# A second triangular inverse kept beside the first in an RWKV-7 chunk kernel: products on TensorE in place of transposes on VectorE

## The reference

```python
def rwkv7_scan(r, w, k, v, kk, a):
    def step(state, inp):
        r_t, w_t, k_t, v_t, kk_t, a_t = inp
        sa = jnp.einsum('bhvk,bhk->bhv', state, -kk_t)
        state = (state * w_t[:, :, None, :] + sa[..., None] * (kk_t * a_t)[:, :, None, :]
                 + v_t[..., None] * k_t[:, :, None, :])
        return state, jnp.einsum('bhvk,bhk->bhv', state, r_t)
    ...
# for each direction d (d = 1 on flipped sequences):
        o = rwkv7_scan(*ins)
        bonus = jnp.sum(rh * kd * r_k.astype(F32), axis=-1, keepdims=True) * vh
        dir_out.append((group_norm(o, gn_w, gn_b) + bonus.reshape(nB, S, D)) * g.astype(F32))
```

## Time and profile before

| | |
|---|---|
| median of three runs | 2423.7 us (2422.42 to 2425.13) |
| the profiled execution, its span | 2422.42 us, 2420.5 us |
| busy: TensorE, its weight loads | 2271.3 us (94%), 1695.2 us (70%) |
| busy: VectorE, ScalarE, GpSimd | 1254.5 (52%), 948.3 (39%), 829.2 (34%) us |
| the eight passes of `pair` | 906.7 to about 1392 us of the span, 485 us |

### The profile page before, as it was taken

One profiled execution on the slowest core, in us unless ns is written; L12 is line 12 of the kernel. 1 busy time (PEld: TensorE's weight loads), 2 busy tenths in 40 slices (PEclk: granted clock), 3 DMA queues, 4 the chain that ended last, 5 costly groups with the idle time before them and its releaser, 6 DMA issues.

```text
span 2420.5 us, 45998 instructions
## 1 busy us (share of the span) xinstructions
PE 2271.3 (94%) x19396; PEld 1695.2 (70%) x19396; DVE 1254.5 (52%) x2027; ACT 948.3 (39%) x1665; POOL 829.2 (34%) x456
## 2 busy tenths in 40 slices
PE   8999999999978998888888898999998999999998
PEld 6886778888866647777777747877887766763476
DVE  5128254022164476777777515595313899736123
ACT  4238434233244434454445434465322222344133
POOL 2310334344413124444444203344441433330246
PEclk9999999999979998999999999999997999999999
DMA  4312222232312210000000112244221333222222
GB/s 143 118 51 77 70 70 87 104 96 82 101 36 67 96 41 10 7 8 10 8 9 10 38 61 71 94 182 139 96 87 61 131 113 113 87 87 79 70 89 85
DMA packets 49883, 180.69 MB, mean 75 GB/s; under 512 B 5601, under 2 KB 5857, under 8 KB 49441
## 3 DMA queue, kind: packets, MB, share of 16 engines
q1 hardware_dynamic: 46064, 166.89, 21.0%
q10 hardware_dynamic: 3632, 11.08, 1.1%
HBM read 167.39 MB, written 10.55 MB: 74 GB/s over the span
## 4 chain that ended last, share of the span: by engine, by line
PE 72%; issue 12%; DVE 6%; ACT 6%; POOL 3%; DMA 1%; POOLq 0%; ACTq 0%; SPq 0%; DVEq 0%
PE ps L596 15%; PE ps L597 15%; PE ps L598 14%; PE ps L599 6%; POOL ring_lo L2202 3%; PE ps L895 3%; PE ps L858 2%; PE ps L644 2%; PE ps L886 1%; PE ps L806 1%; PE ps L1072 1%; PE ps L715 1%; ACT arena L1453 1%; PE ps L1008 1%; PE ps L730 1%
## 5 line engine op out<-in xcount | busy, mean ns | idle before, releaser
L2202 POOL TENSOR_TENSOR ring_lo<-ring,ring_hi 128x1024 fp32r<-128x1024 f32 x232 | 565.2, 2444 | 1017.7 <-ACT ring_hi L1129 1017.6
L598 PE MATMUL ps<-u_lo,ring_hi 128*128 128x512 f32 x968 | 384.8, 398 | 0.0
L1129 ACT ACTIVATE ring_hi<-ring 128x1024 fp32r<-128x1024 f32 x232 | 243.1, 1053 | 108.4 <-DMA ring<-in_wall 105.0
L599 PE MATMUL ps<-arena,ring 128*128 128x512 f32 x608 | 266.1, 594 | 6.3 <-ACT arena L1573 3.3
L599 PEld LDWEIGHTS ps<-arena,ring 128*128 128x128 f32 x608 | 114.4, 190 | 154.2 <-issue 138.5
L596 PE MATMUL ps<-mlp_u_hi,ring_hi 128*128 128x512 f32 x512 | 204.9, 400 | 13.0 <-DVE u_lo L1690 8.5
L598 PEld LDWEIGHTS ps<-u_lo,ring_hi 128*128 128x128 f32 x968 | 183.8, 190 | 43.4
L596 PE MATMUL ps<-mid_hi,ring_hi 128*128 128x512 f32 x512 | 203.4, 397 | 2.6 <-POOL ring_lo L2202 2.6
L597 PE MATMUL ps<-mlp_u_hi,ring_lo 128*128 128x512 f32 x512 | 203.7, 398 | 0.0
L598 PE MATMUL ps<-mid_lo,ring_hi 128*128 128x512 f32 x512 | 202.6, 396 | 0.0
L597 PE MATMUL ps<-mid_hi,ring_lo 128*128 128x512 f32 x512 | 202.6, 396 | 0.0
(11 more groups left out here) (423 smaller groups left out, 4296.5 us busy)
## 6 DMA issues: line engine op xcount, KB each, us to landing
ring<-in_wall SPq DMA_DIRECT2D x273, 512.0 KB, 3.6
s_tables<-arena ACTq DMA_DIRECT2D x16, 512.0 KB, 2.9
arena<-s_tables SPq DMA_DIRECT2D x16, 512.0 KB, 3.6
arena<-bias_lines SPq DMA_DIRECT2D x16, 448.0 KB, 4.2
arena<-in_lora SPq DMA_DIRECT2D x8, 384.0 KB, 2.9
h<-in_x SPq DMA_DIRECT2D x1, 2048.0 KB, 8.1
out<-arena ACTq DMA_DIRECT2D x8, 256.0 KB, 2.9
consts<-in_consts SPq DMA_DIRECT2D x1, 1216.0 KB, 14.2
```

What stands on the lines that cost most here:

```text
L598: return nc.tensor.matmul(y, w_hi, low, start=False, stop=x == k - 1)
L599: return nc.tensor.matmul(y, ring[:, at:at + P], rhs(x), start=x == 0, stop=x == k - 1)
L1129: nc.scalar.activation(ring_hi[:, slot], ring[:, slot], ACT.Copy).then_inc(sem("weights_high"), 1)
L2202: G.tensor_tensor(ring_lo[:, slot], ring[:, slot], ring_hi[:, slot].bitcast(F32), ALU.subtract).then_inc(sem("weights_split"), 1)
```

## The change

TT is no longer made by transposing T. It is kept as a second matrix with its own additions: at each level but the last, a further half product X.TT (stationary X, columns of TT) goes into bank C, and VectorE adds it to TT from there. At the start T and TT are each set to the unit matrix by GpSimd and then receive their level-0 entries by a conditional copy (`copy_predicated`) from PSUM, T from a new product A (features be and al crossed), TT from L's product in B. Since C is then in use at each level, the hidden products and the stacked products move to bank A, and X, which goes there too, gets waits for what was read from A last.

```diff
-                pe.wait_ge(sem("z_taken"), n(6, 6))
                 for d in range(2):
                     pe.wait_ge(sem("features_v"), n(2, d + 1))
                     pe.wait_ge(sem("features_p"), n(2, d + 1))
+                    each_crossed(A[d], F[d]["be"], F[d]["al"]).then_inc(sem("scores_ready"), 1)
+                pe.wait_ge(sem("z_taken"), n(6, 6))
+                for d in range(2):
                     each_crossed(B[d], F[d]["al"], F[d]["be"]).then_inc(sem("scores_ready"), 1)
...
+                        if nxt and l in (2, 3):
+                            pe.wait_ge(sem("z_taken"), nxt(6, k - 1))
+                        if l == 4:
+                            pe.wait_ge(sem("masked_v"), n(6, 2 * d + 4))
+                        if l == 5:
+                            pe.wait_ge(sem("turned"), n(4, 2 * d + 2))
                         each(A[d], R[d]["LM"], R[d]["T"]).then_inc(sem("x_ready"), 1)
...
                         each_half(B[d], R[d]["TT"], R[d]["X"], l, 1 - d).then_inc(sem("dt_ready"), 1)
+                        if l < LEVELS - 1:
+                            each_half(C[d], R[d]["X"], R[d]["TT"], l, d).then_inc(sem("dtt_ready"), 1)
...
-                                hidden_product(nxt, l - 1, other, 2)
+                                hidden_product(nxt, l - 1, other, 0)
...
-                            each_stacked([C[d], O[d]], F[d], F[d]["ro"]).then_inc(sem("scores_ready"), 1)
+                            each_stacked([A[d], O[d]], F[d], F[d]["ro"]).then_inc(sem("scores_ready"), 1)
...
# VectorE
+                for d in range(2):
+                    dve.wait_ge(sem("scores_ready"), n(11, 1 + d))
+                    dve.wait_ge(sem("t_filled"), n(2, d + 1))
+                    placed("T", 0, "level_n", d).then_inc(sem("t_started"), 1)
                 for d in range(2):
                     dve.wait_ge(sem("l_copied"), n(2, d + 1))
                     dve.wait_ge(sem("tt_filled"), n(2, d + 1))
-                    V_.copy_predicated(chunks(R[d]["TT"]), mask("level", d * LEVELS).bitcast(mybir.dt.int32),
-                                       chunks(R[d]["L"])).then_inc(sem("tt_started"), 1)
+                    placed("TT", 1, "level", d * LEVELS).then_inc(sem("tt_started"), 1)
-                for d in range(2):
-                    dve.wait_ge(sem("tt_started"), n(2, d + 1))
-                    V_.transpose(R[d]["T"], R[d]["TT"]).then_inc(sem("t_started"), 1)
...
                         if l < LEVELS - 1:
-                            dve.wait_ge(sem("t_updated"), n(10, k + 1))
-                            V_.transpose(R[d]["TT"], R[d]["T"]).then_inc(sem("t_turned"), 1)
+                            dve.wait_ge(sem("dtt_ready"), n(8, k + 1))
+                            old, new = [columns_of_level(a, l, d) for a in (R[d]["TT"], bank(4 * d + 2))]
+                            TT(old, old, new, ALU.add).then_inc(sem("tt_updated"), 1)
...
# GpSimd
+                    for d in range(2):
+                        pool.wait_ge(sem("u_ready"), n(16, 15 + d))
+                        units("T", d)
```

More of the change, by code:

```diff
@@ L931, in pair @@
                         k = 2 * (l - 1) + d
[L932 to L933 removed]
+                        if l == 1:
+                            pe.wait_ge(sem("tt_started"), n(2, d + 1))
+                            pe.wait_ge(sem("masked_v"), n(6, d + 1))
+                        else:
+                            pe.wait_ge(sem("tt_updated"), n(8, k - 1))
                         pe.wait_ge(sem("x_taken"), n(10, k + 1))
                         each_half(B[d], R[d]["TT"], R[d]["X"], l, 1 - d).then_inc(sem("dt_ready"), 1)
+                        if l < LEVELS - 1:
+                            each_half(C[d], R[d]["X"], R[d]["TT"], l, d).then_inc(sem("dtt_ready"), 1)
                         if nxt and l <= 2 and d == 0:
@@ L1482, in pair @@
                         for d in range(2):
-                            act.wait_ge(sem("scores_ready"), n(9, 7 + d))
-                            taken(F[d]["ka"], bank(4 * d + 2), "turned")
+                            act.wait_ge(sem("scores_ready"), n(11, 9 + d))
+                            taken(F[d]["ka"], bank(4 * d), "turned")
                             taken(F[d]["be"], bank(4 * d + 3), "turned")
                     if l == 5:
-                        act.wait_ge(sem("scores_ready"), n(9, 9))
+                        act.wait_ge(sem("scores_ready"), n(11, 11))
                         for e in range(2):
@@ L1991, in pair, with placed @@
                 F, G = feats[parity], feats[1 - parity]
+                def placed(name, b, kind, i):
+                    return V_.copy_predicated(chunks(R[d][name]), mask(kind, i).bitcast(mybir.dt.int32), chunks(bank(4 * d + b)))
+                for d in range(2):
+                    dve.wait_ge(sem("scores_ready"), n(11, 1 + d))
+                    dve.wait_ge(sem("t_filled"), n(2, d + 1))
+                    placed("T", 0, "level_n", d).then_inc(sem("t_started"), 1)
                 for d in range(2):
@@ L2022, in pair @@
                         for d in range(2):
-                            dve.wait_ge(sem("scores_ready"), n(9, 5 + d))
-                            for name, b in (("M0", 2), ("M1", 3)):
+                            dve.wait_ge(sem("scores_ready"), n(11, 7 + d))
+                            for name, b in (("M0", 0), ("M1", 3)):
                                 TT(chunks(R[d][name]), chunks(bank(4 * d + b)), mask("incl", d), ALU.mult
@@ L2243, in features, with units @@
                         G.tensor_tensor(r["ka"], r["ka"], r["kd"], ALU.mult).then_inc(sem("features_p"), 1)
-            def units(d):
+            def units(name, d):
                 eye = const("eye", 0, CH).unsqueeze(1).to_broadcast([P, NCH, CH])
-                G.tensor_copy(chunks(R[d]["TT"]), eye).then_inc(sem("tt_filled"), 1)
+                G.tensor_copy(chunks(R[d][name]), eye).then_inc(sem("t_filled" if name == "T" else "tt_filled"), 1)
             def pair(parity, n, prev, nxt):
@@ L2265, in pair @@
                         pool.wait_ge(sem("dt_ready"), n(10, 9 + d))
-                        units(d)
+                        units("TT", d)
                     features(nxt, feats[1 - parity], 1)
-                    pool.wait_ge(sem("scores_ready"), n(9, 9))
+                    pool.wait_ge(sem("scores_ready"), n(11, 11))
                     stage_v(nxt)
+                    for d in range(2):
+                        pool.wait_ge(sem("u_ready"), n(16, 15 + d))
+                        units("T", d)
             first = lambda per, c=0: c
@@ L2276, in _ @@
             stage_v(first)
-            for d in range(2):
-                units(d)
+            for name in ("TT", "T"):
+                for d in range(2):
+                    units(name, d)
             over_pairs(pair)
```

19 lines of the change are left out of this document (5 added, 14 removed).

## The result

The changed kernel takes 2485.7 us (median of 4, 2484.4 to 2486.2) against 2423.1 on the same chip: 1.0261 of before, 95% interval 1.0248 to 1.0273, slower by 63 us. The prediction was 2493 with a range of 2466 to 2512. Times of runs are medians; one of the twelve executions of e11 took 11,271.7 us, which nothing explains, and its ratio leaves it out.

A forecast was written before the change was run, and what follows sets the result against it. TensorE, busy 94% of the span, was taken as the bound, with instruction supply deciding levels 3 and 4. Terms 1.9 + 2.0 + 0.9 + 3.9 = 8.7 us a pass, +69.6 over eight, gave 2493 us, range 2466 to 2512.

The forecast's parts named there:

- the scores: Start of a pass: six groups ahead of the variances in place of four, TensorE being the bound, +1.9 us a pass.
- level 1: Two new groups X.TT that follow their neighbours without overlap, no slack on TensorE: +2.0 us a pass.
- Rival (4): Half groups and added score groups run side by side with their partners: -1.0 us a pass, 2416 us; chance 0.03.
- The transposes: Transposes of 0.71 us behind each addition in the levels, said to be off TensorE's way to the next X.
- Conditional copies: Start of a pass: VectorE's four copies hidden behind six groups, variances and X, 0; at most +1.9 us.
- level 5 and the scan: Level 5 already on ScalarE's path, the scan with the same instructions: 0 for each.
- level 2: Two new groups, +2.0 us, less the vanishing wait of 1.02 us for VectorE: +0.9 us a pass.
- The slower of the two decides: 18.5 for 14.6, +3.9: Levels 3 and 4: TensorE's own sum with waits, 17.2 to 17.8 us, against instruction supply, 18.5 us; the slower counts.
- the floor of five blocks: Levels 3 and 4: instruction supply of five blocks of 256 at 3.7 us each, 18.5 us.
- rival (3): Slower still: blocks at 4.2 us, late conditional copies or more half clock; some +11 us a pass, 2512 us; chance 0.11.
- Rival (1): New groups first fill TensorE's 4.9 us of idle time before the scan: +5.0 us a pass, 2464 us; chance 0.09.
- Rival (2): Instruction fetch stays hidden, levels 3 and 4 take 17.3 us: +7.5 us a pass, 2484 us; chance 0.08.

The follow-up runs named there:

- e11: Kernel before with exponentials moved into the scan, direction 1's turning product into level 5, logarithms behind the copies of L: 2416.6 us, ratio 0.9973.
- e1: Changed kernel without the two added score groups and GpSimd's fills of T; T started by transposing TT, as before: 2470.2 us, ratio 1.0192.
- e3: Changed kernel with the crossed half of level 3's stacked products left out, 128 instructions fewer a pass: 2479.3 us, ratio 1.0236.
- e10: Changed kernel with each direction's masks M0 and M1 made right after that direction's additions in level 3: 2478.5 us, ratio 1.0242.
- e2: Changed kernel without the ten new groups, TT transposed from T again, moved banks and their waits kept: 2441.1 us, ratio 1.0073.
- e6: Kernel before with direction 1's exponentials behind level 5's copies of X, VectorE's sums split between levels 1 and 2, bonus products in level 4: 2421.3 us, ratio 0.9987.
- e9: Kernel before with VectorE's sums split, exponentials moved into the scan, direction 1's turning product into level 5: 2419.3 us, ratio 0.9992.
- e12: Kernel before with VectorE's sums split, exponentials in the scan, direction 1's turning product in level 5, logarithms behind the copies of L: 2410.5 us, ratio 0.9948.

## Why the prediction was right, and where it wasn't

Right, with the mechanism shown: TensorE was the bound of the scores and of level 1, a plain group costs 0.93 to 0.99 us, and there is no overlap of a half group with its partner (1.98 for two). e1 removed two groups and got their time back. Rival (4), side by side, is out. The transposes were off the path: in the trace before TensorE waits 0.6 us in eight passes for those at the start of T and not at all for the others, so freeing 30 us of VectorE gave nothing to speak of. Conditional copies, fills of T, level 5 and the scan cost nothing, as forecast.

Mis-sized: the scores, +1.66 for 1.9 (crossed groups follow each other at 0.93 to 0.99, and 0.15 us of idle time before level 1 went), and level 2, +0.67 for 0.9, since a level of six plain groups and two wide products is 6.84 us and not 7.1.

Wrong in its mechanism though near in its size: the step "The slower of the two decides: 18.5 for 14.6, +3.9" for levels 3 and 4. Measured were 18.6 for 14.1, +4.5; the 14.6 was read from the sixth pass alone, in which the two levels took longest of the six. I took TensorE's own sum and the supply of instructions as alternatives over both levels. They add up instead, level by level: level 3 is work plus two waits (9.36, the same with 128 instructions fewer in e3), level 4 is 8.3 us with 1.5 us of stops (gone in e3). What the change added to the two levels is four groups of work (in the sixth pass 12.4 us busy to 16.2) and the mask wait of 0.84, both of which stood in the prediction's own sum, and not stops, which became fewer. e10 brought both levels to 18.0, below the floor of five blocks that I had set. That the floor and the measured mean agree to 0.1 us is luck. A block isn't 3.7 us everywhere: it was 3.57 to 4.22 in the traces before and 3.85 here.

Where the 69.6 us forecast became 64.0: 3.1 in the first pass, 2.2 in the six middle ones, 0.3 in the last. The first pass is the stretch at half clock: no term held it, rival (3) had it come more often, and it came less often. In a middle pass the scores and levels 1 and 2 took 0.55 less than forecast, levels 3 and 4 0.63 more, level 5 and the scan 0.45 less. The other 1.3 us between 2493 and 2485.7 lie within the scatter of the executions.

Rival (1), filled gaps (+5.0 a pass), failed as argued: TensorE's idle time shrank by 7 us and not by 39 (8 x 4.9). Rival (2), no limit of supply, is refuted by the stops in level 4 and by e3, although its time of 2484 was closer to the measured one than mine. That was chance: its +7.5 was too little for a middle pass (+8.33) and too much for the first (+5.6).

What stays open: what the half clock costs apart from the stages, why its spells come and go, and why the stops in level 4 vary from pass to pass (level 4 of e3 still took from 7.75 to 9.3 us).

## What to carry to other kernels

Before moving work from an idle engine to a busy one, look for the wait that the work to be removed ends: the eight transposes of 0.71 us a pass in the levels ended none, while ten groups of 0.96 us landed on the bound. A product that reuses a PSUM bank brings the reader of that bank into the path; in e2, where nothing else filled the time, that was 2.3 us a pass, and 0.7 in the changed kernel. A stop before one engine often hides a later one of another: split sums gave nothing in e6, cost 0.3% in e9, and gave 0.25% in e12 once ScalarE's logarithms had been moved. And a stage made shorter is not yet a pass made shorter: of the 2.8 us that e12 took out of the levels the scan took back 1.8.

## What the hardware showed that I hadn't expected

TensorE can run out of instructions, and then it stands still where the program has no wait. The packets of 16 KB rose from 91 to 111 over the eight passes, 20 x 256 = 5120 instructions, exactly the 8 x 640 that ten groups of 64 add:

```profile
q8 instruction: 111, 1.82, 1.4%
```

The times of these packets in the trace fit the stops. Around the two of level 4 they are seen in slices of 0.2 us (1285 to 1293 us):

```profile
GB/s 0 0 0 0 0 82 0 0 0 0 0 0 0 0 0 0 0 0 0 0 0 0 0 0 82 0 0 0 0 0 0 0 0 0 0 0 0 0 0 0
```

One packet starts at 1286.07 us and takes 1.27, the next at 1289.93 and takes 1.29; TensorE goes on at 1288.67 and 1292.52, 1.3 us after each has ended. All stops of more than 0.35 us in the passes do the same, 21 in the kernel before and 14 in the changed one: TensorE goes on 1.25 to 1.56 us after the end of a packet, and the next packet starts 1.0 to 2.4 us after that. A stop thus ends behind a block that has come, and the packet of the next block starts only after TensorE has gone on.

Stacked products, which do twice the matmuls in the same engine time, use twice the instructions, and 12 of the 21 stops in the changed kernel end at their line (L886). The stops became fewer with the change although 5120 instructions were added: the added groups are plain ones, at 64 instructions in about 0.96 us.

Conditional copies with their data in PSUM took 714 to 743 ns, all 32. With both operands in SBUF nine of 16 took 727 to 744 and seven 1785 to 1799. GpSimd is recorded as busy throughout in those seven, but also in one of the nine (727 ns, at 910.24 us) and in eight of the 32 (735 to 743 ns). So its work alone doesn't make the copy slow; what does isn't shown.
